# Twenty of 48 modulation groups moved from TensorE to VectorE in a two-network diffusion block kernel

## The reference, cut to what matters

```python
for layer in range(4):
    shift, scale, gate    = split(silu(c)     @ mod_w[layer] + mod_b[layer])    # 2048 x 6144
    cshift, cscale, cgate = split(silu(c_ctx) @ mod_w[layer] + mod_b[layer])
    h     = rms_norm(x,   norm_g) * (1 + scale)  + shift
    h_ctx = rms_norm(ctx, norm_g) * (1 + cscale) + cshift
    y, y_ctx = mixer[layer](h, h_ctx)          # in-projection, mixer, out-projection
    x   = x   + gate  * y
    ctx = ctx + cgate * y_ctx                  # not in layers 1 and 3
```

## Time and profile before

| | before |
|---|---|
| median of 3 runs | 2985.89 us (2984.72 to 2990.39) |
| profiled execution, its time | 2983.98 us |
| profiled execution, its span | 2982.3 us |
| mean granted TensorE clock | 0.974 of full speed |
| PE busy | 2835.7 us, 95% of the span |
| DVE busy | 1450.8 us, 49% |
| ACT busy | 1210.2 us, 41% |
| POOL busy | 284.2 us, 10% |
| read from HBM | 481.37 MB |

### The profile page before, as it was taken

How to read it: one execution, slowest core, us unless ns; L and a number is a source line. 1 busy time by engine, 2 the same in 40 slices (tenths; PEclk the granted TensorE clock), 3 DMA queues, 4 the chain that set the end, 5 groups by cost and what they waited for, 6 DMA issues and landing times.

```text
span 2982.3 us, 43033 instructions
## 1 busy us (share of the span) xinstructions
PE 2835.7 (95%) x15346; PEld 2215.5 (74%) x15346; DVE 1450.8 (49%) x2016; ACT 1210.2 (41%) x1871; POOL 284.2 (10%) x401
## 2 busy tenths in 40 slices
PE   5899999999899999999998899999999898999989
PEld 2366666678677777777777777777887687998879
DVE  4355454553454646556565622333454424555664
ACT  3254544542334444434344432322444323553652
POOL 1100000012200000000002400000000123000000
PEclk8799999999999999999999999999999998899999
DMA  9756556533254545455544355452212132453325
GB/s 370 303 212 216 213 202 218 210 117 115 93 198 171 191 174 191 162 181 178 184 160 140 128 194 194 172 199 90 93 62 80 52 110 92 142 183 118 125 96 169
DMA packets 106521, 484.52 MB, mean 162 GB/s; under 512 B 12240, under 2 KB 14288, under 8 KB 81616
## 3 DMA queue, kind: packets, MB, share of 16 engines
q1 hardware_dynamic: 74176, 267.49, 25.5%
q0 software_dynamic: 32272, 216.02, 20.4%
HBM read 481.37 MB, written 2.10 MB: 162 GB/s over the span
## 4 chain that ended last, share of the span: by engine, by line
PE 88%; DMA 3%; DVE 3%; ACT 3%; issue 2%; DVEq 0%; ACTq 0%; POOL 0%; POOLq 0%; SPq 0%
PE psum L237 24%; PE psum L239 23%; PE psum L238 23%; PE psum L251 5%; DMA y<-in_mod_weights 2%; PE psum L596 2%; PE psum L274 1%; DVE h_lo L368 1%; PE psum L787 1%; PE psum L1284 1%; PE psum L830 1%; PE psum L1298 1%; ACT w_hi L211 1%; PE psum L801 1%; DMA y<-in_x_rows 1%
## 5 line engine op out<-in xcount | busy, mean ns | idle before, releaser
L237 PE MATMUL psum<-h_hi,w_hi 128*128 128x512 f32 (+1 forms) x3840 | 1370.0, 357 | 42.9 <-DVE h_lo L368 38.8
L239 PE MATMUL psum<-h_hi,w_lo 128*128 128x512 f32 (+1 forms) x3840 | 1331.9, 347 | 0.0
L238 PE MATMUL psum<-h_lo,w_hi 128*128 128x512 f32 (+1 forms) x3840 | 1331.7, 347 | 0.0
L219 DVE TENSOR_TENSOR w_lo<-raw,w_hi 128x1024 fp32r<-128x1024 f32 x496 | 588.4, 1227 | 662.6 <-ACT w_hi L211 660.5
L237 PEld LDWEIGHTS psum<-h_hi,w_hi 128*128 128x128 f32 x3840 | 732.5, 191 | 201.5 <-issue 76.9
L238 PEld LDWEIGHTS psum<-h_lo,w_hi 128*128 128x128 f32 x3840 | 734.2, 191 | 89.4 <-issue 6.5
L239 PEld LDWEIGHTS psum<-h_hi,w_lo 128*128 128x128 f32 x3840 | 733.0, 191 | 90.9
L211 ACT ACTIVATE w_hi<-raw 128x1024 fp32r<-128x1024 f32 x496 | 496.8, 1052 | 406.6 <-PE psum L239 396.0
L257 POOL DMA_DIRECT2D modraw<-in_mod_weights x160 | 84.7, 529 | 1400.2 <-PE psum L251 1390.3
L251 PE MATMUL psum<-modraw,cond 128*32 128x512 f32 x1408 | 199.4, 643 | 10.4 <-DVE mod L281 5.9
L544 DVE SCALAR_TENSOR_TENSOR y<-psum,mod,work 128x256 f32 (+1 forms) x32 | 15.5, 484 | 211.9 <-PE psum L239 207.8
(11 more groups left out here) (240 smaller groups left out, 2484.9 us busy)
## 6 DMA issues: line engine op xcount, KB each, us to landing
raw<-in_weights SPq DMA_DIRECT2D x496, 512.0 KB, 4.6
modraw<-in_mod_weights POOLq DMA_DIRECT2D x176, 1024.0 KB, 5.2
y<-in_mod_weights POOLq DMA_DIRECT2D x16, 1024.0 KB, 8.7
work<-in_gate_w POOLq DMA_DIRECT2D x16, 256.0 KB, 5.1
work<-in_x_t POOLq DMA_DIRECT2D x16, 256.0 KB, 3.7
xl<-in_x_rows SPq DMA_DIRECT2D x1, 2048.0 KB, 9.7
y<-in_x_rows SPq DMA_DIRECT2D x1, 2048.0 KB, 16.6
y<-in_ctx_t POOLq DMA_DIRECT2D x1, 2048.0 KB, 11.0
```

The source lines that it names most:

```text
L219: dve.tensor_tensor(w_lo[:, par, half, :], raw[:, 2 * par + half, :], w_hi[:, par, half, :].bitcast(F32), ALU.subtract).then_inc(S["split_ ...
L237: pe.matmul(dst, hi, h_hi[:, k, 0:n], start=(k == 0), stop=False)
L238: pe.matmul(dst, hi, h_lo[:, k, 0:n], start=False, stop=False)
L239: mm = pe.matmul(dst, lo, h_hi[:, k, 0:n], start=False, stop=(k == KT - 1))
```

## The change

Twenty of the 48 groups are no longer made on PE: layer 0's gate, layer 1's shift and scale, layer 3's shift and gate. They become 80 units of one tile (128 outputs), made on DVE. A unit loads its tile's 1 MB of weights with the outputs on the partitions and the 2048 inputs in the free dimension (`unit_load`, by POOL, in two halves of 512 KB into one buffer, `mw_work` or `mw_sgu`), and multiplies it with a row of silu(c) that is the same on all partitions and sums along the row: one SCALAR_TENSOR_TENSOR (STT) of 128x1024 with `accum_out` per half and condition, four in all, then a tiny STT that adds the halves and the bias. The latent product goes to PSUM banks 6 and 7 as junk, the context product over the weights. `unit_lat` makes the latent sum only, with two STTs.

Where the units stand:

- LRU blocks: two per block, one behind the split of the next u strip, one behind the output `y` (32).
- Output stage 0: one behind each of the 16 tiles.
- Output stage 2: none behind tiles 0 and 1, two behind tiles 2 and 3, one behind each of the other twelve.
- Last SGU: two latent units behind `vn` in each of the 8 groups.

The condition rows (2 MB per network) are loaded by POOL into the modulation buffer (`cb_load`), ACT takes the tanh (`cb_tanh`), DVE finishes the silu (`cb_silu`): before the first LRU block, and around tile 1 of output stage 2. The remaining PE groups are made at the start (8), in attention (16) and in groups 0 to 3 of the first SGU (4). `norm_pe` waits for the units, since the junk lies in its bank.

```diff
+        def cb_load(pool, net):
+            for s in range(2):
+                pool.dma_start(cb[:, s, :], ins["cond_rows"][2 * net + s]).then_inc(modraw_in[s], 16)
+        def cb_tanh(act, net):
+            for n in range(4):
...
+                act.activation(mw_work[:, half, :], cb[:, s, half * 1024:(half + 1) * 1024], ACT.Tanh, scale=0.5).then_inc(S["cond_tanh"], 1)
+        def cb_silu(dve, net):
+            for n in range(4):
...
+                dve.scalar_tensor_tensor(out=part, in0=mw_work[:, half, :], scalar=1.0, in1=part,
+                                         op0=ALU.add, op1=ALU.mult).then_inc(S["cond_ready"], 1)
+            dve.wait_ge(S["cond_ready"], 4 * net + 5)
+        def unit_load(pool, p, mw):
+            for half in range(2):
+                ge(pool, S["unit_used"], 2 * p + half - 1)
+                pool.dma_start(mw[:, half, :], ins["mod_units"][2 * p + half]).then_inc(unit_in[half], 16)
+        def unit(dve, p, par, slot):
+            for half in range(2):
+                dve.wait_ge(unit_in[half], 16 * (MOD_FIRST + p + 1))
+                ge(dve, S["junk_done"], 2 * p + half)
+                part = slice(half * 1024, (half + 1) * 1024)
+                dve.scalar_tensor_tensor(out=junk, in0=mw_work[:, half, :], scalar=0.5, in1=cb[:, 0, part], op0=ALU.mult,
+                                         op1=ALU.mult, accum_out=macc[:, par, 0, half:half + 1]).then_inc(S["junk_done"], 1)
+                dve.scalar_tensor_tensor(out=mw_work[:, half, :], in0=mw_work[:, half, :], scalar=0.5, in1=cb[:, 1, part], op0=ALU.mult,
+                                         op1=ALU.mult, accum_out=macc[:, par, 1, half:half + 1]).then_inc(S["unit_used"], 1)
+            dve.wait_ge(S["unit_used"], 2 * p + 2)
+            dve.scalar_tensor_tensor(out=mod[:, bass.ds(slot, 1), :], in0=macc[:, par:par + 1, :, 0], scalar=col("mod_b", slot),
+                                     in1=macc[:, par:par + 1, :, 1], op0=ALU.add, op1=ALU.add).then_inc(S["unit_cols"], 1)
+            dve.wait_ge(S["unit_cols"], p + 1)
+        def unit_lat(dve, p, par, slot):
...
         def norm_pe(pe, l):
             pe.wait_ge(S["sq_added"], added_base[l + 1])
+            ge(pe, S["unit_used"], 2 * UNITS_READY[l])
...
         def out_pool(pool, l):
             if l in fetched:
                 pool.wait_ge(y_sem[l], y_count[l])
+                if l == 2:
+                    cb_load(pool, 1)
                 for c in range(2):
                     fetch(c, c, True)
+                if l == 2:
+                    pool.wait_ge(S["cond_ready"], 9)
+                    unit_load(pool, U_OUT2, mw_work)
...
                     add(2 * j + c, c, False)
                     if l in fetched:
                         fetch(2 * j + 2 + c, c, False)
+                    units(2 * j + c)
...
         def lru_pe(pe):
-            strip(pe, su, psum[:, U_BANK, :], NT, between=lambda half: mod_chunk(pe, M_LRU + b, half),
+            strip(pe, su, psum[:, U_BANK, :], NT,
...
-                mod_turn(pe, M_LRU + b, 0)
...
         def lru_dve(dve):
                 next_strip(split_lo, dve, su)
+                unit(dve, 2 * b, 0, GATE + b)
...
-                mod_add(dve, M_LRU + b)
...
                 low(12, OUT_REST)
+                unit(dve, 2 * b + 1, 1, 3 * KT + SCALE + b)
...
         def sgu_dve(dve, lay):
                     ins_.then_inc(G["vn"], 1)
+                    if lay == 1:
+                        for u in range(2):
+                            unit_lat(dve, U_SGU + 2 * i + u, u, 9 * KT + GATE + 2 * i + u)
```

More of the change, by code:

```diff
@@ new lines, in unit_lat @@
+        def unit_lat(dve, p, par, slot):
+            for half in range(2):
+                dve.wait_ge(unit_in[half], 16 * (MOD_FIRST + p + 1))
+                dve.scalar_tensor_tensor(out=mw_sgu[:, half, :], in0=mw_sgu[:, half, :], scalar=0.5, in1=cb[:, 0, half * 1024:(half + 1) * 1024],
+                                         op0=ALU.mult, op1=ALU.mult, accum_out=macc[:, par, 0, half:half + 1]).then_inc(S["unit_used"], 1)
+            dve.wait_ge(S["unit_used"], 2 * p + 2)
+            dve.scalar_tensor_tensor(out=mod[:, bass.ds(slot, 1), 0:1], in0=macc[:, par:par + 1, 0:1, 0], scalar=col("mod_b", slot),
+                                     in1=macc[:, par:par + 1, 0:1, 1], op0=ALU.add, op1=ALU.add).then_inc(S["unit_cols"], 1)
+            dve.wait_ge(S["unit_cols"], p + 1)
@@ L534, in out_dve, with tile @@
                     op0=ALU.add, op1=ALU.mult).then_inc(S["mod_a_done"], 1)
-            def tile(j, c, last):
+            def tile(j, c, last, first=False):
                 st = Strip(out_strip[l], c, j)
@@ L550, in tile @@
                     next_strip(split_lo, dve, st)
-            with dve.Fori(0, KT // 2 - 1) as j:
+                if l == 0:
+                    unit(dve, U_OUT0 + m, c, 3 * KT + SHIFT + m)
+                if l == 2:
+                    for n in range(0 if first else 2 if isinstance(j, int) and j == 1 else 1):
+                        q = 2 * c + n if isinstance(j, int) and j == 1 else m
+                        unit(dve, U_OUT2 + q, q % 2 if isinstance(q, int) else c, 9 * KT + SHIFT + q)
+            if l == 2:
+                for c in range(2):
+                    tile(0, c, False, True)
+                cb_silu(dve, 1)
+                for c in range(2):
+                    tile(1, c, False)
+            with dve.Fori(2 if l == 2 else 0, KT // 2 - 1) as j:
                 for c in range(2):
@@ L570, in block @@
                 pool.dma_start(lw["gw"][par], ins["gate_w"][b].rearrange("p (g d) -> p g d", g=4)).then_inc(gw_in[par], 16)
-                for q in range(2 if isinstance(b, int) and b == 0 else 0, 4):
-                    mod_load(pool, M_LRU + b, q)
-            for q in range(2):
-                mod_load(pool, M_LRU, q)
+                if not first:
+                    for n in range(2):
+                        unit_load(pool, 2 * b + n, mw_work)
+            pool.wait_ge(S["mod_used"], 4 * MOD_FIRST)
+            cb_load(pool, 0)
             pool.wait_ge(S["hf_done"], KT)
@@ L578, in lru_pool @@
                 block(b, b, True)
+            pool.wait_ge(S["cond_ready"], 5)
+            for p in range(4):
+                unit_load(pool, p, mw_work)
             with pool.Fori(1, BLOCKS // 2) as j:
@@ L659, in lru_dve @@
             dve.wait_ge(S["pads_zero"], 1)
+            cb_silu(dve, 0)
             def block(j, par, last=False):
@@ L842, in body @@
                     mm.then_inc(A["v_t"], 1)
-                    mod_turn(pe, M_ATT + i, 1)
-            rounds(pe, body, HEADS1, 2)
+                    mod_turn(pe, M_ATT + i, 0 if isinstance(i, int) and i < 4 else 1)
+            rounds(pe, body, HEADS1, 2, 4)
         def att_act(act):
@@ L1004, in sgu_pool, with units @@
             mods = lay == 0
+            def units(g):
+                if not mods:
+                    for n in range(2):
+                        unit_load(pool, U_SGU + 2 * g + n, mw_sgu)
             def table(g, par, first):
```

130 lines of the change are left out of this document (96 added, 34 removed).

## The result

The changed kernel takes 2969.74 us (median of 7 runs, 2967.83 to 2978.65) where the kernel before takes 2987.36 beside it (7 runs, 2984.72 to 2993.05). The ratio is 0.9944, interval 0.9931 to 0.9958: 17 us faster, which is over the 6 us that a measurement tells. 2960 was forecast. The profiled execution took 2970.66 us with a span of 2969.0.

What follows compares the result with a forecast made beforehand. TensorE, busy 95%, was taken as the bound, with VectorE becoming it in LRU blocks. Terms -56.7 + 4.9 - 26 + 19.4 + 33 = -25.4 us gave 2960 us; own case 2935 to 2985, range for all 2920 to 3005.

Steps and rivals of the forecast that it cites:

- the sum of -25.4 us: Whole kernel: the stage terms -56.7, +4.9, -26, +19.4 and +33 added, taking the span from 2982.3 to 2956.9 us.
- TensorE's loss in the LRU blocks and VectorE as the new bound: LRU blocks: TensorE sheds 5.6 us per block, VectorE becomes the bound; -56.7 us up to output stage 0.
- U: VectorE's time for one whole unit, four STTs plus tail: 5.4 us, bounds 5.1 and 5.9.
- 27.4 against 25.4: LRU block: VectorE needs 27.4 us with two units, TensorE alone would need 25.4.
- Half rate with an accumulator: Rival, all units: accumulating STTs take 2.24 us each, about +190 us, 3177 us; chance 0.10.
- The last unit ahead of the norm: Norm behind output stage 0, again behind stage 2: TensorE's normalization waits for the last unit, +4.9 us each.
- "0.8": Norm behind output stage 0: sums of squares started 0.8 us after the last gated tile; subtracted in the +4.9.
- First SGU: First SGU of network 2, groups 4 to 7: TensorE loses modulation chunks and turn, 6.5 us each, -26 us.
- Output stage 2: Residual behind condition rows and single-buffered double units delay TensorE: +12, clock +2.5; with the norm's +4.9, +19.4 us.
- Last SGU: Pair of half units delays Z's split: groups 21.7 us, +27 in seven, +6 for clock; +33, bounds +7 and +47.
- The half units and the single buffer cost more: Rival: slower landing, low clock in every last SGU group and U = 5.9; +13 us, 2999 us; chance 0.17.
- DVE does nothing more here: First SGU of network 2: VectorE gets no added work, so the -26 us was called the surest term.

Runs made afterwards that it cites:

- Run 9: Changed kernel with the 32 LRU units multiplying only 8 of each 1024 columns, loads kept: 2952.6 us, 0.9881 of the kernel before.
- Run 4: Changed kernel with unit products of both out projections in PSUM banks 2 and 3, the norm's wait for units removed: 2957.8 us, 0.9901 of the kernel before.
- run 5: Changed kernel with the 16 half units moved from the last SGU to the first SGU's last four groups: 2929.3 us, 0.9811 of the kernel before.
- after: The kernel with the whole change, measured against the kernel before: 2969.7 us, ratio 0.9944.
- run 2: Changed kernel with a buffer for each of the two half units of a last SGU group: 2952.5 us, 0.9893 of the kernel before.
- run 7: Changed kernel with the last SGU's half units loading fully but multiplying only 8 of each 1024 columns: 2957.0 us, 0.9896 of the kernel before.
- run 6: Changed kernel with the last SGU's half units loading only 128 of 1024 columns per half, products kept: 2947.1 us, 0.9867 of the kernel before.

## Why the prediction was right

The direction and most mechanisms stood, and the time lies inside the stated range; the sum of -25.4 us came out as -13.3 in the traces and 17 us in the medians. That it missed by no more is partly luck: the terms were off by -7.0 in the LRU stage and -2.3 in the first SGU, and by +4.4 and +5.0 at the two norms, +3.1 between them and +8.9 in the last SGU.

- **TensorE's loss in the LRU blocks and VectorE as the new bound**: right. U was 5.16 for 5.4 and a block 26.98 for 27.4, which makes 6.3 us in 15 blocks; -63.7 was measured for -56.7. Run 9 shows both sides of "27.4 against 25.4".
- **Half rate with an accumulator**: it had no row for it, and none came: 1.15 us.
- **The last unit ahead of the norm**, +4.9: the wait was right (5.6 us for 5.7), the term mis-sized, +9.3 and +9.9. The "0.8" misread: it is the wait ahead of the last eight of 24 products. The other sixteen used to run ahead of it and now come behind the unit, 2.94 - 1.07 = 1.9 us; and behind 6.6 us of idling all 24 run at the lower clock, 2.3 more. The prediction used that effect in the last SGU and not here. Run 4 took both out.
- **First SGU**, -26: -28.3.
- **Output stage 2**, +12 and +2.5: +14.6, by the mechanism named (residual behind the condition rows, a load between double units). That it agrees to 0.1 us is chance: TensorE waited 4.0 us for the first tile and once, 5.3 us, for the double units, where the forecast had 4.5, 2.3 and 5.2, and the rest is the lower clock behind both waits (0.74 and 0.50). It missed that the third tile's residual is queued behind GpSimd's wait for those rows.
- **Last SGU**, +33: +41.9. The mis-sized terms are the pair, 9.4 for 8.7, and the clock, in all groups in place of half: 13.0 + 9.4 + 2.05 = 24.4 us by the prediction's own layout, 24.1 measured. The rival named for it (*The half units and the single buffer cost more*) named the low clock in every group, and in this stage that is what came; its other terms did not.
- "**DVE does nothing more here**", said of the first SGU as the reason for its surest term, was also where the units should have stood: run 5.

Not settled: why TensorE was granted less clock in the first attention head of after alone, and what the last SGU would cost with all its loads issued in time; the four groups of run 2 say little, but no kernel shows it for the whole stage.

## What to carry to other kernels

Work moved to an engine with a low average is free only at a place where that engine is idle and nobody waits behind it: the same 16 half units cost 42 us in one stage and nothing measurable in another, and more than half of a norm's delay (5.4 of 9.3 us) was a PSUM bank that a unit shared with it. Before adding a buffer, look at what the load is queued behind, and weigh a piece of work by its length with the waits inside it. And price a new wait of TensorE with the lower clock behind it, also where only small products follow.

## What the hardware showed beside this

**VectorE and GpSimd take turns.** Both engines in output stage 0 of after:

```profile
660.01 2.33 POOL L582 TENSOR_TENSOR work<-work 128x512 f32<-128x512 f32 x1 [2.05 <-ACT work L540]
661.10 2.33 DVE L334 SCALAR_TENSOR_TENSOR psum<-work,modraw 128x1024 f32<-128x1024 f32 x1
662.30 1.59 POOL L584 TENSOR_TENSOR y<-xl,small  x1
663.35 0.14 DVE L334 DVE_READ_ACCUMULATOR psum<-work,modraw 128x1 f32 x1
663.35 1.62 DVE L336 SCALAR_TENSOR_TENSOR work<-work,modraw 128x1024 f32<-128x1024 f32 x1
```

VectorE's product starts while GpSimd's addition runs, 1.2 us before its end, and ends 1.1 us behind it; GpSimd's next operation, 0.61 us before the change, takes 1.59 under the product; and VectorE's second product again loses 0.4 us to it. The Trainium skill ("SBUF — State Buffer", "SBUF: two separate sides") says that such a pair shares SBUF ports under an exclusive lock, held for the whole instruction, and the trace agrees: each slow duration is the rest of the other's instruction plus its own. It costs VectorE 1.5 us per tile, hidden in stage 0, where TensorE's 10.9 us per tile are more than VectorE's 10.3.

**The accumulator read** (0.14 and 0.08 us) lies under the next product and costs nothing; ScalarE's entry of 195 ns, taken as a bound, was no guide.

**Loads by GpSimd beside SP's weights**: 512 KB landed in 4.7 us (median, last SGU of after), in 5.8 in run 7, and in 7.4 and 9.6 in run 2, where four were issued at once and a stretch of 4 us showed 419 GB/s. 64 KB landed in 2.3 us (run 6).
